# Third mixer's last selection: ten rounds of 8 keys spread over attention units 0 to 17, nine closing steps over units 18 to 20

## The reference

```python
def dsa_sparse_attention(q, k, v, iq, ik, iw):
    n_blk = S // Q_BLOCK                      # 512 / 128 = 4 blocks of queries
    top_k = min(TOPK_MAX, S // 4)             # 128
    key_chunk = jnp.arange(S) // CHUNK        # chunks of 64 keys
    def block(i):
        ...
        admissible = key_chunk[None, :] <= q_chunk[:, None]
        rel = jax.nn.relu(jnp.einsum('bthd,bsd->bths', iq_b, ik_f) * (IDX_DIM ** -0.5))
        score = jnp.einsum('bths,bth->bts', rel, iw_b)
        score = jnp.where(admissible[None], score, -jnp.inf)
        _, idx = lax.top_k(score, top_k)
        ...
        logits = jnp.einsum('bthd,btkhd->bthk', q_b, k_sel).astype(jnp.float32) * (dh ** -0.5)
        ...
        p = jax.nn.softmax(logits, axis=-1).astype(v.dtype)
        return jnp.einsum('bthk,btkhd->bthd', p, v_sel)
```

## Time and profile before

| what | value |
|---|---|
| median of the 3 runs | 3363.08 us |
| the runs | 3363.08, 3358.32, 3368.62 us |
| the profiled execution, its time | 3371.58 us |
| the profiled execution, its span | 3369.5 us, mean granted TensorE clock 0.970 |
| PE's first scores (L1985) to the first output copy (L2801) | 2841.95 to 2932.07 us |
| PE, DVE, ACT, POOL busy over the span | 95, 47, 33, 35% |

### The profile page before, as it was taken

One profiled execution on the slowest core, in us unless ns is written; L12 is line 12 of the kernel. 1 busy time (PEld: TensorE's weight loads), 2 busy tenths in 40 slices (PEclk: granted clock), 3 DMA queues, 4 the chain that ended last, 5 costly groups with the idle time before them and its releaser, 6 DMA issues.

```text
span 3369.5 us, 62902 instructions
## 1 busy us (share of the span) xinstructions
PE 3203.9 (95%) x25706; PEld 2430.5 (72%) x25706; DVE 1567.7 (47%) x2342; ACT 1108.9 (33%) x1561; POOL 1170.5 (35%) x589
## 2 busy tenths in 40 slices
PE   7999999979899999999999999989999899999999
PEld 5757888848688886777766756448887774448887
DVE  6755553184255555677230421445052667536060
ACT  5413433212433333434233313232222333422121
POOL 3333444414144322444433412014444255014443
PEclk9999999979899999999999999999999889999999
DMA  3212333313000002555322212113332112012333
GB/s 131 80 43 82 96 98 100 106 50 97 17 3 3 3 3 73 180 185 186 128 98 85 87 63 75 38 57 100 94 100 88 57 62 71 1 63 94 100 94 100
DMA packets 74609, 268.58 MB, mean 80 GB/s; under 512 B 8719, under 2 KB 8730, under 8 KB 74240
## 3 DMA queue, kind: packets, MB, share of 16 engines
q1 hardware_dynamic: 73536, 262.53, 24.3%
q0 software_dynamic: 896, 3.52, 0.3%
HBM read 261.71 MB, written 2.10 MB: 78 GB/s over the span
## 4 chain that ended last, share of the span: by engine, by line
PE 75%; issue 10%; DVE 7%; POOL 4%; ACT 3%; DMA 0%; POOLq 0%; DVEq 0%; SPq 0%; ACTq 0%
PE gp L388 53%; POOL w_low L357 4%; PE gp L1227 4%; PE gp L2174 2%; PE gp L314 2%; PE gp L2696 2%; PE aux L1353 1%; PE aux L1227 1%; PE gp L1985 1%; PE gp L2648 1%; PE aux L1994 1%; DVE arena L1667 1%; DVE aux L2863 1%; PE aux L1222 1%; PE aux L2596 1%
## 5 line engine op out<-in xcount | busy, mean ns | idle before, releaser
L357 POOL TENSOR_TENSOR w_low<-ring,w_high 128x1024 fp32r<-128x1024 f32 x397 | 955.9, 2409 | 1840.5 <-ACT w_high L326 1840.5
L326 ACT ACTIVATE w_high<-ring 128x1024 fp32r<-128x1024 f32 x397 | 420.2, 1059 | 1351.3 <-PE gp L388 1292.9
L388 PE MATMUL gp<-ffn_h,w_high 128*128 128x512 f32 x2432 | 757.6, 393 | 12.5 <-DVE ffn_h L418 5.0
L388 PEld LDWEIGHTS gp<-ffn_h,w_high 128*128 128x128 f32 x2432 | 455.2, 189 | 123.0 <-POOL w_low L357 12.6
L388 PE MATMUL gp<-ffn_h,w_low 128*128 128x512 f32 x1216 | 475.0, 391 | 0.0
L388 PE MATMUL gp<-ffn_high,w_high 128*128 128x512 f32 x928 | 362.1, 390 | 3.4 <-POOL w_low L357 3.3
L388 PE MATMUL gp<-ffn_low,w_high 128*128 128x512 f32 x864 | 336.6, 390 | 0.0
L388 PE MATMUL gp<-ffn_high,w_low 128*128 128x512 f32 x864 | 336.6, 390 | 0.0
L388 PEld LDWEIGHTS gp<-ffn_h,w_low 128*128 128x128 f32 x1216 | 229.3, 189 | 48.4
L2102 DVE TENSOR_TENSOR arena<-arena 128x512 f32<-128x512 f32 x64 | 152.9, 2389 | 200.2 <-ACTq L163 200.2
L388 PE MATMUL gp<-in_h,w_high 128*128 128x512 f32 x768 | 239.4, 393 | 4.5 <-DVE in_h L416 4.5
(11 more groups left out here) (474 smaller groups left out, 5093.8 us busy)
## 6 DMA issues: line engine op xcount, KB each, us to landing
ring<-in_weights SPq DMA_DIRECT2D x437, 512.0 KB, 3.6
H<-in_ada SPq DMA_DIRECT2D x48, 512.0 KB, 4.3
arena<-arena SPq DMA_DIRECT2D x32, 67.5 KB, 2.0
X<-in_x SPq DMA_DIRECT2D x4, 512.0 KB, 7.4
out_x<-X SPq DMA_DIRECT2D x8, 256.0 KB, 4.4
arena<-in_sm POOLq DMA_DIRECT2D x1, 1024.0 KB, 5.1
cst<-in_cst SPq DMA_DIRECT2D x1, 756.0 KB, 9.8
arena<-in_hy_f_w POOLq DMA_DIRECT2D x1, 512.0 KB, 5.1
```

Of the source, the lines that this page charges most:

```text
L326: nc.scalar.activation(w_high[:, slab % PARTS, :], ring[:, slab % RING, :], ACT.Copy).then_inc(high_ready, 1)
L357: nc.gpsimd.tensor_tensor(w_low[:, slab % PARTS, :], ring[:, slab % RING, :], w_high[:, slab % PARTS, :], ALU.subtract).then_inc(low_ready, 1)
L388: last = nc.tensor.matmul(gp[:, t.bank, :], wt[:, slab % PARTS, w], x(k), start=(k == 0 and q == 0), stop=(k == sum(kt) - 1 and q == 2))
```

## The change

Only the table in `three_dve` that says which unit carries which piece of the last selection (L2944 to L2948). The pieces, their operands, their order and their count are the same; no instruction is added or taken out, on any engine, and no DMA is moved. Before, units 0 to 9 have a round each, units 10 to 13 two closing steps each and unit 14 the last one. Now units 0, 2, 4, 6, 8, 10, 12, 14, 16 and 17 have a round each, and units 18, 19 and 20 three closing steps each.

```diff
+            ROUND_UNITS = (0, 2, 4, 6, 8, 10, 12, 14, 16, 17)
+
             def beside(u):
-                if u < 10:
-                    rounds(3, 5 + u, 6 + u)
-                elif u < 15:
-                    select(3, range(2 * u - 20, min(2 * u - 18, 9)))
+                if u in ROUND_UNITS:
+                    k = 5 + ROUND_UNITS.index(u)
+                    rounds(3, k, k + 1)
+                elif 18 <= u < 21:
+                    select(3, range(3 * u - 54, 3 * u - 51))
 
             attention_dve(dve, v, DSA, beside)
```

## The result

| what | before | changed |
|---|---|---|
| median | 3359.12 us (20 runs) | 3368.18 us (20 runs) |
| lowest to highest | 3352.87 to 3371.56 us | 3359.5 to 3377.0 us |
| ratio, changed to before | | 1.0020, 95% interval 1.0011 to 1.0030 |
| profiled span (of one execution) | 3369.5 us | 3373.0 us |

In microseconds the ratio is +6.7 (3.7 to 10.1); it is taken over all the runs, and the two medians by themselves lie 9.06 us apart. The change makes the kernel a little slower, by less than the 0.3% that one measurement can tell.

A forecast was written before the change was run, and what follows sets the result against it. PE, busy for 95% of the span, was taken to bound the kernel. Terms of 0 + 0 - 0.2 + 3.95 us made +3.7 us, which on the median of three runs gave 3367 us, range 3360 to 3375.

The forecast's parts named there:

- Odd units 1, 3 and 5: Third mixer's attention: rounds taken out of these units are hidden ones, so removing them gains 0 us.
- Units 0 and 6 keep their waits: Both units keep their rounds, so PE's waits stay, including 1.3 us ahead of unit 7's transposes: 0 us.
- Units 7 to 15: Closing steps leave, rounds come to units 10, 12 and 14: net -0.2 us, between -0.5 and +0.2.
- the 0.15 for unit 9: Within units 7 to 15: about 0.15 us put as saved for unit 9, whose round leaves.
- Units 16 to 20: Rounds in 16 and 17, closing steps in 18 to 20: DVE sets the pace and PE loses 3.95 us.
- The sum, +3.7: All terms for the attention stage together: the kernel 3.7 us slower, none of it caught up later.
- Rival D: Units 16 to 20: DVE's pieces hide in its idle half, no cost, 3363.1 us; chance 0.05.
- the rule of the Trainium skill: Judging engines by occupancy over the whole span, moving DVE's work is free, so the sum would be 0.
- Rivals A and B: New gaps, units 17 to 21, lower PE's clock: once (A), 3370.2 us, chance 0.2; twice (B), 3373.6 us, chance 0.05.
- Rivals C and E: Low clock in units 7 to 9 goes (C, 3363.4 us, 0.05); all 2.9 us of waits go too (E, 3360.8, 0.03).
- the same 3.7 on the median: The 3.7 us worked out on the profiled execution was added unchanged to the three-run median, giving 3366.8 us.

The follow-up runs named there:

- changed again: The changed kernel with nothing altered, run a second time beside the kernel before; ratio 1.0012 (0.9997 to 1.0028), attention stage 92.94 us.
- before third: The kernel before with nothing altered, run and profiled a third time; ratio 1.0003 (0.9988 to 1.0017), attention stage 95.53 us.
- before again: The kernel before with nothing altered, run and profiled a second time; ratio 0.9997 (0.9982 to 1.0012), attention stage 88.87 us.
- the kernel with both units cleared: Kernel before with rounds moved to units 1 to 5 and 7 to 11, none in 0 and 6, closing steps in 12 to 18; ratios 0.9987 and 0.9992.
- the one with unit 6 cleared: Kernel before with rounds in units 0 to 5 and 7 to 10, none in 6, closing steps in 11 to 15; ratio 0.9987 (0.9973 to 1.0002).

## Why the prediction was right, and where it was off

The time was put at 3367 us and came out at 3368.18, within the range and within 0.3% of before. That the two lie 1.4 us apart is luck: the sum started from a median of three runs, 3363.08, where twenty gave 3359.12, so its start was 4.0 us too high; and it added 3.7 where the medians differ by 9.06. What holds is the mechanism and its size at equal clock. By its steps:

- *Odd units 1, 3 and 5: 0.* Right, and shown by leaving the rounds out: 22.70 us to unit 7 with and without. In the changed kernel again it is 22.71, with pairs of 4.87 us as put. Under the long low pattern the order was worth a little: 25.21 and 25.18 us to unit 7 in the changed kernel, 25.39 in before third.
- *Units 0 and 6 keep their waits.* Right: 0.86 and 1.27 us in the changed profile.
- *Units 7 to 15: -0.2.* It was 0.0: unit 15's transposes come 47.15 us after the first scores in changed again and 47.16 in before again. Rounds in units 10 and 12 cost 0.17 and 0.18 from start to start, and 0.44 was saved behind unit 12, as put. What was not there is the 0.15 for unit 9: the pace from unit 9 to 10 is 2.79 us in both. Units 12 and 15 came 0.06 and 0.03 us later from start to start, which the text had not put.
- *Units 16 to 20: +3.95.* From unit 15's to unit 22's transposes 20.19 us in changed again against 16.11 in before again (rows below the list), 4.08 more. By units, late by 0.99, 0.42, 0.32, 1.27 and 0.98, and 0.1 more in units 16 and 22; the text had 0.97, 0.44, 0.34, 1.22 and 0.98. Nothing was caught up behind (25.60 us from unit 22 to the end of the stage in both), and PE did not wait for the mask.
- *The sum, +3.7.* At equal clock 4.0 (4.07 and 3.98): 0.2 from the term for units 7 to 15, 0.1 from that for 16 to 20.
- *Rival D, and the rule of the Trainium skill beside it* ("Perfetto Trace Analysis", "Identifying the Most-Contended Engine"), read over the whole span: 0. The five extra rounds on a half-idle DVE cost 2.71 us. In units of 384 keys with a piece beside them DVE is the busiest engine (14.29 of 15.3 us in the changed profile, PE 12.36), so the rule holds if it is read for these fifteen microseconds, and misleads over the span.
- *Rivals A and B.* The clock did not fall behind the new gaps: none of the three profiles of the changed kernel has a low stretch in the stage later than 39 us after the first scores, and the new gaps come at 51 us or later. Their price was off too: the 6.8 us of low clock of the earlier trace rows cost 90.12 - 87.27 = 2.85 us, not 3.4, and one fall can also last 3.4 or 13.7 us.
- *Rivals C and E.* Unit 6's gap stayed, and so did a low stretch at it in all three profiles of the changed kernel; PE's waits grew by 2.6 us instead of going.
- *The low clock.* The step that fell is the sentence "the same 3.7 on the median" together with the low stretch of the earlier trace rows taken as fixed. It is one of several patterns: 3.4, 6.8 and 20.5 us of low clock in the kernel before, 3.4 and 20.5 in the changed one, none in two kernels that keep the same gap.

Timeline of PE, transposes of units 15 and 22, changed again and then before again:

```profile
2893.20 0.44 PE L2010 MATMUL gp<-cst,arena 128*128 128x128 f32 x2
...
2913.39 0.49 PE L2010 MATMUL gp<-cst,arena 128*128 128x128 f32 x3
```

```profile
2886.25 0.38 PE L2010 MATMUL gp<-cst,arena 128*128 128x128 f32 x2
...
2902.36 0.49 PE L2010 MATMUL gp<-cst,arena 128*128 128x128 f32 x3
```

The part of the measured +6.7 us that is over 4.0 is open. The intervals of all three comparisons contain 1.0012, which is what 4.0 us make, so no further cause is needed, and none is ruled out. Whether the changed order also makes long runs more likely is not settled: 24 of its 44 timed runs lie over 3367, and 14 over 3371, which is the same line moved by 4 us. In the same three comparisons 17 of 90 runs of the kernel before lie over 3367. That is 32% against 19%, which so few runs do not tell apart.

## What to carry to other kernels

Side work on an engine with idle time is free only up to that engine's room in the very unit that carries it; compare pace with pace (here 1.26 us of DVE work against 2.33 of PE, so 1.07 of room and no more), not busy shares over a span. In the first unit that carries such work even less of it counts: of a round of 1.51 us only 0.52 was covered there, and PE came 0.99 late. When two engines hand work back and forth with a depth of two, find which pieces stand in the loop before thinning them out: here every second round of units 1 to 5 was hidden, and removing those gave nothing. And before subtracting two profiles of TensorE-bound kernels, see that they have the same granted clock in the stretch compared.

## What the hardware showed that I had not expected

One program shows several patterns of low clock in the same stage from run to run. The kernel before had 3.4, 6.8 and 20.5 us of it in its three profiles, the changed one 3.4 and twice 20.5. The low time can outlast the gap that it follows by far: after the 1.27 us gap at unit 7, PE worked 13.72 of 14 us and the clock stayed at 0.51 for nearly all of them, while in another profile of the same kernel it was back after 3.5 us. The Trainium skill, in "TensorE: Matmul & The Clock Gate", Part 1, lets the gate follow how busy PE was recently; the fall after the gap agrees with that, and the 14 us of low clock with PE busy throughout are not explained by it here. Why it lasts 3.4, 6.8 or 13.7 us was not tried.

The stage's price for low clock also depends on where it falls: 3.4 us of it at 23 us cost 88.87 - 87.27 = 1.60 us, while 3.4 us at 1 to 5 us, where PE mostly waits for ACT's first exponentials, cost some 0.4 by an estimate that rests on the expected values: the kernel with both units cleared was expected 1.85 - 1.2 = 0.65 us shorter than the one with unit 6 cleared, and came out 86.11 - 85.86 = 0.25 shorter (85.86 is the mean of its two profiles), with that stretch against none. No pair of profiles shows that price by itself.
